# Three-branch attention in pairs of heads on the halves of TensorE, with the division by the row sums on GpSimd

## What is computed

```python
# 16 heads of width 64 in 4 groups of 4; a group shares keys and values. T = 512
o_cmp = softmax(q . k_cmp) . v_cmp        # compressed blocks, made before the stage in question
o_slc = softmax(q . k_slc, causal) . v_slc    # top_n = min(16, 8) = 8 of 8 blocks: all causal keys
o_win = softmax(q . k_win, causal) . v_win    # window 512: all causal keys
o = g[0] * o_cmp + g[1] * o_slc + g[2] * o_win    # g = sigmoid gates, one per token, head and branch
```

## Time and profile before

| what | value |
|---|---|
| median of 3 runs | 3922.49 us (3922.02 to 3939.49) |
| the profiled execution, its own time | 3925.23 us |
| its span (first to last instruction) | 3923.4 us |
| PE busy | 3527.5 us, 90% of the span |
| DVE, ACT, POOL busy | 46%, 34%, 29% of the span |
| mean granted clock | 0.935 |

### The profile page before, as it was taken

One profiled execution on the slowest core, in us unless ns is written; L12 is line 12 of the kernel. 1 busy time (PEld: TensorE's weight loads), 2 busy tenths in 40 slices (PEclk: granted clock), 3 DMA queues, 4 the chain that ended last, 5 costly groups with the idle time before them and its releaser, 6 DMA issues. The chain is left out here.

```text
span 3923.4 us, 50300 instructions
## 1 busy us (share of the span) xinstructions
PE 3527.5 (90%) x16751; PEld 2796.5 (71%) x16755; DVE 1817.4 (46%) x3883; ACT 1317.0 (34%) x2206; POOL 1150.8 (29%) x667
## 2 busy tenths in 40 slices
PE   5979889899979999999988858999888789989988
PEld 4856676799978888888875535688766644468876
DVE  5504324877747777777744584211012155521101
ACT  3223433245533333333332324233121134433312
POOL 1312342288812222222211101244332100034432
PEclk7879999999989999999998979999998879999999
DMA  4330232245589999999822100233223300023321
GB/s 96 82 73 17 62 99 71 63 161 182 179 294 323 322 325 325 321 323 322 319 65 57 44 27 22 65 95 91 74 62 71 88 31 25 0 75 91 96 74 60
DMA packets 459491, 507.19 MB, mean 129 GB/s; under 512 B 76912, under 2 KB 401808, under 8 KB 441440
## 3 DMA queue, kind: packets, MB, share of 16 engines
q1 hardware_dynamic: 436064, 369.09, 31.0%
q0 software_dynamic: 18432, 134.23, 9.3%
q10 hardware_dynamic: 4864, 2.23, 0.3%
HBM read 458.07 MB, written 38.80 MB: 127 GB/s over the span
## 5 line engine op out<-in xcount | busy, mean ns | idle before, releaser
L124 POOL TENSOR_TENSOR w_low<-w_ring,w_high 128x1024 fp32r<-128x1024 f32 (+2 forms) x264 | 615.4, 2338 | 1702.6 <-ACT w_high L119 1702.6
L135 PE MATMUL ps<-h_low,w_high 128*128 128x512 f32 x1600 | 654.0, 409 | 132.1 <-POOL w_low L124 103.9
L136 PE MATMUL ps<-h_high,w_high 128*128 128x512 f32 x1600 | 641.3, 401 | 0.0
L137 PE MATMUL ps<-h_high,w_low 128*128 128x512 f32 x1600 | 639.8, 400 | 0.0
L135 PEld LDWEIGHTS ps<-h_low,w_high 128*128 128x128 f32 x1600 | 308.3, 193 | 223.9 <-POOL w_low L124 118.8
L135 PE MATMUL ps<-h_low,u_high 128*128 128x384 f32 x1024 | 352.2, 344 | 51.0 <-POOL u_low L124 41.6
L119 ACT ACTIVATE w_high<-w_ring 128x1024 fp32r<-128x1024 f32 (+2 forms) x264 | 263.3, 1012 | 299.7 <-PE ps L137 254.7
L136 PEld LDWEIGHTS ps<-h_high,w_high 128*128 128x128 f32 x1600 | 308.4, 193 | 72.5 <-issue 3.3
L137 PEld LDWEIGHTS ps<-h_high,w_low 128*128 128x128 f32 x1600 | 307.8, 192 | 72.6
L137 PE MATMUL ps<-h_high,u_low 128*128 128x384 f32 x1024 | 348.3, 340 | 0.0
L136 PE MATMUL ps<-h_high,u_high 128*128 128x384 f32 x1024 | 348.0, 340 | 0.0
(11 more groups left out here) (465 smaller groups left out, 6411.6 us busy)
## 6 DMA issues: line engine op xcount, KB each, us to landing
w_ring<-in_peer_uv_dram SPq DMA_DIRECT2D x128, 512.0 KB, 5.6
u_raw<-in_peer_uT_dram SPq DMA_DIRECT2D x80, 512.0 KB, 5.8
w_ring<-in_peer_uT_dram SPq DMA_DIRECT2D x48, 512.0 KB, 3.6
peer_gates<-ring SPq DMA_DIRECT2D x12, 2048.0 KB, 7.4
gates<-peer_gates SPq DMA_DIRECT2D x32, 768.0 KB, 10.6
w_ring<-in_ffn_w_gate_dram SPq DMA_DIRECT2D x44, 512.0 KB, 3.8
w_ring<-in_ffn_w_up_dram SPq DMA_DIRECT2D x44, 512.0 KB, 3.8
w_ring<-in_w_in_dram SPq DMA_DIRECT2D x36, 512.0 KB, 3.9
```

Source lines behind the costliest of these rows:

```text
L124: return eng.tensor_tensor(rounded(low), whole, high, ALU.subtract)
L135: nc.tensor.matmul(out, rounded(w_high), rounded(x_low), start=start, stop=False, **more)
L136: nc.tensor.matmul(out, rounded(w_high), rounded(x_high), start=False, stop=False, **more)
L137: return nc.tensor.matmul(out, rounded(w_low), rounded(x_high), start=False, stop=stop, **more)
```

## The change

A new function `paired_attention` takes the place of `attention` for this mixer alone; the other three callers of `attention` keep it. Its unit is a *pair*: the two heads of a query tile in one branch, 16 pairs in all, written out without a hardware loop. In the diff `a` (0 or 1) is the head of the pair.

- TensorE issues the two heads' score products next to each other (`pair["scores"](a)`: one on rows 0 to 63, one on rows 64 to 127, into two PSUM banks), then both masks. There are two pairs of score banks instead of three single ones. The two heads' products in `weigh` also stand next to each other, one into each half of bank 7, and so do the two of the compressed branch.
- The operands are read where they lie (`qT`, `kT`, `vs`, `vw`, `pcT`, `vcr`); the staging DMAs are gone.
- DVE takes both reciprocals at once (128x2) and multiplies them by both gates (a new TENSOR_TENSOR, 128x2). GpSimd multiplies the probabilities by the result, except for head 1 at t = 3, which DVE does (`on_dve`).
- The copies out of PSUM: t = 0 both heads at once on DVE, t = 1 both at once on ACT, t = 2 and 3 one head on each. They go through three banks in turn.

The cases under `mixed` are for another caller and are not used here (`"mix"` is in no pair).

```diff
+def paired_attention(c, pairs, lag=3):
...
+    score_bank = lambda s, a: 2 * (s % 2) + a
+    pt_banks, out_bank = (4, 5, 6), 7
+    on_dve = lambda t, a: mixed and a == 1 or t == TT - 1 and a == 1
+    kinds = {t: [((0,), ("dve", "dve", "act", "act")[t])] for t in range(TT)} if mixed else {
+        0: [((0, 1), "dve")], 1: [((0, 1), "act")], 2: [((0,), "dve"), ((1,), "act")], 3: [((0,), "act"), ((1,), "dve")]}
...
+                def score(s):
+                    p, t = steps[s]
+                    pair, w = pairs[p], width[t]
+                    if s >= 2:
+                        pe.wait_ge(exped, 2 * (s - 2) + 2)
+                    outs = [c.ps[:, score_bank(s, a), 0:w] for a in range(2)]
+                    for x in range(len(pair["scores"](0))):
+                        for a in range(2):
+                            q, k = pair["scores"](a)[x]
+                            nc.tensor.matmul(outs[a], q[:, t * P:(t + 1) * P], k[:, 0:w], start=x == 0, stop=False)
+                    for a in range(2):
...
+                            mm = nc.tensor.matmul(outs[a][:, w - P:w], c.mask_ident[:, :], c.mask_causal[:, :], start=False, stop=True)
+                        mm.then_inc(scored, 1)
...
+                def turn(s):
+                    p, t = steps[s]
+                    pe.wait_ge(normed_pool, normed_by("pool", s))
+                    if normed_by("dve", s):
+                        pe.wait_ge(normed_dve, normed_by("dve", s))
+                    for g in of_step(s):
+                        if g >= 3:
+                            wait_moved(pe, g - 3, moves[g - 3][2])
+                        for n, a in enumerate(moves[g][1]):
+                            for j in range(t + 1):
+                                at = n * (t + 1) + j
+                                tr = nc.tensor.transpose(c.ps[:, pt_banks[g % 3], at * P:(at + 1) * P], probs[:, s % p_bufs, a, j * P:(j + 1) * P], c.ident[:, :])
...
+                def weigh(p):
...
+                    for j in range(TT):
+                        for a in heads:
+                            mm = nc.tensor.matmul(pair["out"](a)[:, j * P:T], pair["v"](a, j), probsT[:, p % 2, a, j, j * P:T],
...
+            @block.gpsimd
+            def _(pool):
+                for s, (p, t) in enumerate(steps):
+                    for a in range(2):
+                        if not on_dve(t, a):
+                            pool.wait_ge(inverted, s + 1)
+                            of = probs[:, s % p_bufs, a, 0:width[t]]
+                            nc.gpsimd.tensor_scalar(of, of, inverse[:, s % p_bufs, a:a + 1], None, ALU.mult).then_inc(normed_pool, 1)
...
+                def normalise(s):
...
+                    v.reciprocal(inverse[:, n, :], total[:, n, :]).then_inc(summed if gated else inverted, 1)
...
+                    if gated:
+                        dve.wait_ge(summed, s + 1)
+                        v.tensor_tensor(inverse[:, n, :], inverse[:, n, :], pair["gate"](t), ALU.mult).then_inc(inverted, 1)
+                    if on_dve(t, 1):
+                        dve.wait_ge(inverted, s + 1)
+                        of = probs[:, n, 1, 0:width[t]]
+                        v.tensor_scalar(of, of, inverse[:, n, 1:2], None, ALU.mult).then_inc(normed_dve, 1)
...
 def nsa_attention(c, qT, kT, vs, vw, order, pcT, vcr, oT):
...
-        attention(c, KD // TILES, [head(j, b, kind) for j in range(TILES) for b in range(2) for kind in range(2)], 1.0, staging,
-                  {4 * j + 3: (lambda i, j=j: tile_of(oT, i, TILES, j)) for j in range(TILES)})
+    def pair(i, j, kind):
+        half = lambda b: slice(64 * b, 64 * b + 64)
+        tile = TILES * i + j
+        made = dict(scores=lambda b: [(qT[half(b), tile, :], kT[half(b), i + 2 + 2 * kind, :])], mask=None,
+                    v=lambda b, x: (vs, vw)[kind][:, x, i * P + 64 * b:i * P + 64 * b + 64],
+                    gate=lambda t: order[:, t, 1 + kind, 2 * tile:2 * tile + 2],
+                    out=lambda b: c.ps[half(b), 7, :], first=kind == 0, last=kind == 1, sink=oT[:, tile, :] if kind else None)
+        if kind == 0:
+            rows = lambda b: slice(32 * (2 * (j % 2) + b), 32 * (2 * (j % 2) + b) + 32)
+            made["add"] = lambda b: (vcr[rows(b), i, :], pcT[rows(b), 2 * i + j // 2, :])
+        return made
+    paired_attention(c, [pair(i, j, kind) for i in range(KD // TILES) for j in range(TILES) for kind in range(2)])
```

110 lines of the change are left out of this document (added).

## The result

The change takes 3824.07 us (median of 4 runs, 3814.70 to 3824.48); the kernel before, run beside it, takes 3927.62 us (4 runs, 3922.02 to 3939.49). The ratio is 0.9719, with a 95% interval of 0.9692 to 0.9746. The forecast was 3830 us.

The account below looks back on a forecast made before the run. TensorE's own stream was taken to bound the stage. Stream 144, waits 14, ends 4.7 and half clock 9 gave 171.7 us against 263.5, saving 92: 3830 us. Range 3808 to 3867, with 3808 to 3850 given 0.60.

Parts of the forecast that it names:

- forecast's mechanism: Scores and weigh: two heads' half-size products side by side on TensorE overlap fully, costing what one head's cost.
- no overlap: Rival, score pairs between full-size masks and transposes: TensorE keeps 240 us, only 12 to 15 us saved, 3909 us; chance 0.04.
- the second head's passes queue: Rival, score pairs: strict instruction order makes three passes for two, 1.1 us a pair, 17 us, 3847 us; chance 0.10.
- TensorE's stream: TensorE's work in the stage: 16 pairs at 8.5 us plus 8 compressed-branch products at 1.0, 144 us against 240.
- waits of the pairs: TensorE's waits: 0.6 us a pair before transposes of t = 1 plus 0.25 for the DVE-GpSimd conflict, 14 us.
- half clock at the start: Stage start: the first 20 us at half clock were expected again, 9 us lost.
- (1): Sign, whole stage: about 170 us long, with TensorE's pair taking 9 to 10 us.
- (2): Sign, TensorE products: weigh of a pair about 2.4 us; scores of 512 columns for two heads about 1.2 us.
- (3): Sign, GpSimd: its TENSOR_SCALARs take near 0.8 to 1.2 us.
- (4): Sign, TensorE's waits on GpSimd: mostly before transposes of t = 1, near 0.6 us.
- (5): Sign, DVE: its wide multiplication is now and then longer than its 0.55 us.
- (6): Sign, clock: no half-clock stretch in the middle of the stage.

Follow-up runs that it names:

- one head after the other: The change with each head's score followed by its own mask, and weigh doing four products per head in turn: 3900.71 us, 0.9929 of before; stage 235.3 us.
- the wait put back: The change plus seven scratch DMAs of 128x512 that TensorE's first score waits for: 3829.94 us in one run; stage 157.8 us.

## Why the prediction was right, and where it was off

**The forecast's mechanism held.** Halves of TensorE overlap in this mix of forms, within one bank too, and undoing it gives back 82 of the 110 us: 71.5 in the pairs, more changes of form among them, and 10 for the clock and the ends. The rivals "no overlap" and "the second head's passes queue" are out: a lone score pair takes 1.06 us, what a single one takes, where queueing in strict order asked for half as much again. The Trainium skill, page "TensorE: Matmul & The Clock Gate", section "Part 3: Packing small matmuls", has matmuls strictly first in, first out; by that reading a pair would be 1.1 us longer than I took, and the trace does not bear it out. Two of the four instructions of the score pair at 3242.24 are done in 0.70 us together, where the first of a single product takes 0.69 alone (by the profile, which models the ends), so two run side by side. In which order the four were issued, no trace here shows, so whether the engine keeps the order or not stays open.

**The sum, term by term.**

| term | predicted | measured |
|---|---|---|
| TensorE's stream | 144 | 8 x 9.37 + 8 x 8.37 = 141.9 |
| waits of the pairs | 14 | 8 x 0.40 + 8 x 0.42 = 6.6 |
| fill, drain, last read-out | 4.7 | 153.65 - 148.5 = 5.2 |
| half clock at the start | 9 | 0 |
| stage | 171.7 | 153.7 |

- The stream: the 0.15 us for additional weight loads wasn't needed; a window pair is 8.37, which is 7.00 and the 1.4 for masks and transposes.
- The waits: the place was right, the size not. At t = 1 TensorE waits 0.4 us where I had 0.6. GpSimd's 256-column instruction was as I had it (0.92 against 0.93). In the pair shown above the chain from the end of t = 2's masks (3241.26) to the transposes (3244.66) is 3.4 us, where I had 3.7: the hand-overs to DVE and to TensorE take 0.15 and 0.05 us, not 0.2 and 0.2. TensorE's own cover is the 3.0 that I had. The second term, 0.25 us a pair for the conflict, was not there. The conflict itself was, 0.08 to 0.3 us on DVE's wide multiplication and 0.16 on GpSimd's second one of 384 columns, but these belong to t = 2 and t = 3, for which TensorE does not wait in the regular pairs. The other engines' sums held for ACT (6.05 us a pair for 6) and were low for DVE: 6.4 us busy where I had 5.5.
- The clock: I carried the stretch at the start over from before. It is gone, and the run without staging shows that this does not need pairs.
- GpSimd: inside the bounds, but with a slope 2.4 times what I took. My way to the fixed part, from a TENSOR_SCALAR with two operations, overstated the small sizes and understated the large ones. It did not matter, because only t = 1 is on the path and the errors cross near 256 columns.

All that made the stage 18 us better than forecast, and the part behind it was 2.4 us shorter, but the time came out only 6 us better. Two things that no step of the prediction foresaw took the rest. Some 9 us lie ahead of the stage: the medians differ by 103.6 us, where the stage and the part behind it save 112. Another 5 lie in the base: I subtracted from a median of 3922.5 for the kernel before, which a fourth run moved to 3927.6. That 3824 stands so near 3830 is therefore luck in part, and the steps behind the forecast deserve less.

**What the signs were worth.** (1) the stage: 154, not 170; the pair 8.8 to 9.8 us, at the low end of the 9 to 10; (2) `weigh` 2.31 for 2.4, scores 1.06 for 1.2; (3) 0.60 to 1.56 us for 0.8 to 1.2; (4) 0.4 for 0.6; (5) DVE's wide multiplication 0.57 to 0.77 against its 0.55; (6) no half clock in the middle, nor at the start.

**What I had wrong in the design.** The prediction never adds up DVE without GpSimd, and my expectation for that run took GpSimd as needed. It is not. DVE can do it all at 92% busy, 7 us better, because TensorE's regular wait in the change is for GpSimd. And if GpSimd is used, the form with two inputs is better. Between this form and DVE alone, 1.1 us of stage is all there is.

**What stays open.** Why the clock falls in some of these kernels. The granted clock goes to the lower level about 3 us behind the throw-away products in the kernel before (for 20.5 us, in a gap of 3.3), in one head after the other (for 30.7 us, with no gap at all) and with the wait put back (for 3.4 us, behind a gap of 2.9), and 9.8 us behind them with t = 1's multiplication on DVE (for 3.4 us, behind a gap of 1.2). It does so nowhere in the stage of the change, of the old form without staging, of DVE alone and of the two-input form. Every kernel with such a stretch that was traced twice showed the same lengths, so they are set by the instruction stream, but a gap ahead does not tell these kernels apart. Putting the gap back alone brought 1.2 us of loss, not the 9.1 of before. What a stretch costs I can say, what brings it on I can't. Behind the turn of the loop, the turn and the clock are not separated from each other.

## What to carry to other kernels

Where a kernel's bound engine is TensorE and its operands span only half of the rows or columns, put the products of two independent items next to each other, item by item and not batch by batch: the second one was free here in scores (64 rows), in `weigh` (64 columns of one bank) and in parts of 32 rows. Before moving work off an engine, add up that engine in the new pace: DVE at 92% was no bound, and handing its work to the slower engine cost TensorE 0.4 us a pair and relieved nothing that it waited for. Judge a stage by its own first and last row; the rest of this long program moved by up to 9 us from trace to trace of one kernel, while the stage repeated to 0.1.

## What the runs showed of the hardware

- A float32 multiplication on GpSimd by one value a row is slower in the form with a scalar operand than in the form with a broadcast second input: 602, 922, 1318 and 1558 ns against 398, 612, 832 and 1206 at 128, 256, 384 and 512 columns.
- DVE's 128x512 TENSOR_SCALAR and GpSimd's multiplication get in each other's way in both forms. Beside two inputs DVE's takes 968 ns, beside one input 569 (median; 566 to 772), and 486 in the other attentions. In the regular pairs the difference between the first two is where in the GpSimd instruction it begins (0.66 us before its end, or 0.29). The Trainium skill, page "SBUF — State Buffer", section "SBUF: two separate sides", calls the pair of ports an exclusive lock for the whole of a GpSimd instruction. The trace agrees for two inputs: every DVE multiplication ends 0.27 to 0.29 us behind the end of a GpSimd instruction. Beside the one-input form it agrees in 15 of 16 cases in the change, and not in the one of 3227.95, which ends 0.38 us before GpSimd's does; nor in that of 3178.26 in one head after the other, where DVE takes its 0.49 us inside a GpSimd instruction and GpSimd takes 0.24 us more. The page also has a DVE instruction with two SBUF inputs take the lock: the gate product of 128x2 took 161 and 166 ns beside either form, so at this size no run here shows it.
- Half-clock stretches repeated to a tenth of a microsecond in both kernels with such stretches that were traced twice, and one of 30.7 us came with TensorE busy all the time.
